# A fifth class of experts, for at most 64 rows, whose weights are multiplied unsplit in the expert stage of a diffusion step

## The chip, the cores and the metric

The kernel runs on one core of a Trainium2 chip. The time is the device time of one execution in microseconds (us). PE is TensorE, ACT ScalarE, DVE VectorE, POOL GpSimd, and SP the engine whose queue issues the weight loads.

## What is computed

Two layers over 384 rows of width 1024 (128 context rows, 256 latent rows), all in float32. Each layer has a token mixer and a channel mixer. The channel mixer of the first layer is a dense SwiGLU; that of the second is a choice of 2 of 8 experts, each a SwiGLU with inner width 2816:

```python
def swiglu(x, w_gu, w_d):
    g, u = jnp.split(x @ w_gu, 2, axis=-1)
    return (jax.nn.silu(g) * u) @ w_d

def moe_swiglu(x, w_router, w_gu, w_d):
    t = x.reshape(-1, D_MODEL)
    logits = (t @ w_router).astype(jnp.float32)
    top_v, top_i = lax.top_k(logits, TOP_K)
    gates = jax.nn.softmax(top_v, axis=-1)
    ...
    for e in range(N_EXPERTS):
        out = out + combine[:, e:e + 1] * swiglu(t, w_gu[e], w_d[e])
```

The 384 rows make 768 pairs of a row and an expert, so an expert has 96 rows on average, and its number is known only when the router has run.

## The kernel before

**The stream of weights.** All large weights come as one stream of 375 chunks of [128, 2048] float32, 1 MB each, in a fixed order (`STREAM`). SP loads chunk n into slot n % 6 of a ring of six (`raw`), with two DMAs, as soon as PE is done with chunk n - 6 (semaphore `s_pe`). An expert is 33 chunks: 22 of `w_gu` (`N_GU`; gate and up, in blocks of 512 columns, four chunks a block) and 11 of `w_d`. Chunks 111 to 374 of the stream are those of experts 0 to 7.

**Split products.** A float32 product is made of three products of the type float32r: ACT copies a chunk to float32r (`whi`, a ring of three), DVE subtracts that from the chunk in place (`wlo`), and PE multiplies whi by xhi, wlo by xhi and whi by xlo (the helper `three`, lines 1576 to 1578). The splits run two chunks or so ahead of PE (`upto`). The rows' own halves are `xhi`/`xlo` (and `hhi`/`hlo` for the hidden rows).

**Classes of experts.** The program holds each expert in each of four classes, `SHAPES`: (1, 0) is one tile of 128 rows; (1, 1) one tile and up to 32 more rows, the quarter, whose products PE makes unsplit in four column groups of the array (line 2105 for gate and up, 2138 for down); (2, 0) and (3, 0) two and three tiles. DVE counts the rows of each expert and writes the number of the class to `ntile`. PE, ACT and DVE each load it ahead of every expert and compare it with the classes (`by_tiles`). All eight experts of a class stand one behind the other in the program, so that an engine falls through to the next expert where the class stays, and jumps where it changes. The program is entered at the first class's expert 0.

**One expert.** POOL gathers its rows from `h_rows` to `hx`, PE turns them (`gathered`, at down chunks 4 and 6 of the expert before), ACT and DVE make `xhi` and `xlo` of them. Per block: gate and up products in PSUM, ACT's silu, DVE's product (`gated`), PE turns it (line 2072), ACT and DVE split it into `hhi` and `hlo`, and the down products add up over all 22 k-tiles. ACT copies the result to `f` (line 933; for the quarter DVE does), POOL scatters it to `y_rows` and gathers the rows of the expert after the next. `warm(n, bank)` (line 1588) issues n products of the identity with itself, which nothing reads.

## Time and profile before

| | us |
|---|---|
| median of 3 runs (lowest, highest) | 1615.28 (1614.29, 1617.17) |
| the profiled execution | 1618.33 |
| its span, first to last instruction | 1616.6 |
| PE, DVE, ACT busy in the span | 1557.5, 1031.7, 872.7 |
| moved by DMA | 425 MB, mean 263 GB/s |

The profiled execution is 3.05 us longer than the median. Its own span lies 1.7 us under its time. In the rows below, PE's matmuls are pipelined, so their spacing tells more than their length; a float32 product leaves two records in the trace and a split product one each. The chunks' names say nothing of their number, so experts are found by time: expert 0 starts at 759.5 us, expert 1 at 853.5, expert 2 at 947.4, expert 5 at 1228.2, expert 6 at 1321.8, expert 7 at 1459.1.

### The profile page before, as it was taken

The numbers are of one execution on the slowest core, as the hardware profiler recorded it, in microseconds if no ns is written. First come the engines' busy times: TensorE is split into PE (matmuls) and PEld (weight loads), VectorE is DVE, ScalarE is ACT, GpSimd is POOL, SyncE is SP. The second block draws the span as 40 slices with busy tenths as digits, with TensorE's granted clock in tenths as the row PEclk, the third lists the DMA queues.
The fourth block names the chain that finished last, engine by engine and source line by source line (L and its number), as shares of the span: only waits on it lengthen the run. The fifth ranks groups of instructions, "written<-read, shape, count | busy, mean of one in ns | idle before, by whom it ended". The sixth has DMA issues, their size and how long they took to land.

```text
span 1616.6 us, 24317 instructions
## 1 busy us (share of the span) xinstructions
PE 1557.5 (96%) x10076; PEld 1229.6 (76%) x10076; DVE 1031.7 (64%) x935; ACT 872.7 (54%) x886; POOL 164.9 (10%) x180
## 2 busy tenths in 40 slices
PE   6999999999999999998999999999999999999994
PEld 3677777777777778777888888888888878778872
DVE  1445574333422464557888889888888966666665
ACT  2435453222322454545777777777777755555553
POOL 2400000000000220012102030110303010001001
PEclk9999999999999999999999999999999999999998
DMA  9973325666665473233999999999999987878871
GB/s 330 335 264 143 94 84 170 222 210 211 229 241 201 126 246 112 85 125 129 381 371 382 383 367 387 372 379 376 379 383 372 388 323 254 272 265 302 271 283 69
DMA packets 214762, 425.02 MB, mean 263 GB/s; under 512 B 21986, under 2 KB 62946, under 8 KB 214528
## 3 DMA queue, kind: packets, MB, share of 16 engines
q1 hardware_dynamic: 200448, 397.99, 69.4%
q0 software_dynamic: 13056, 22.71, 4.7%
q10 hardware_dynamic: 1136, 2.64, 0.4%
q8 instruction: 84, 1.38, 0.4%
q14 instruction: 38, 0.31, 0.1%
HBM read 418.56 MB, written 22.41 MB: 273 GB/s over the span
## 4 chain that ended last, share of the span: by engine, by line
PE 90%; DVE 4%; DMA 2%; SPq 2%; ACT 1%; issue 1%; POOL 0%; DVEq 0%; ACTq 0%; POOLq 0%
PE ps L1576 26%; PE ps L1578 25%; PE ps L1577 25%; PE ps L2105 3%; PE ps L1620 2%; DMA raw<-in_w_in_dram 1%; SPq L542 1%; PE ps L2138 1%; PE ps L2072 1%; DVE wlo L1072 1%; PE ps L1736 1%; ACT whi L760 1%; PE ps L1767 1%; PE ps L1751 1%; DVE f L1166 1%
## 5 line engine op out<-in xcount | busy, mean ns | idle before, releaser
L1072 DVE TENSOR_TENSOR wlo<-raw,whi 128x2048 fp32r<-128x2048 f32 x327 | 745.4, 2289 | 319.2 <-ACT whi L760 228.1
L760 ACT ACTIVATE whi<-raw 128x2048 fp32r<-128x2048 f32 x327 | 626.6, 1918 | 448.2 <-PE ps L1578 222.1
L1576 PE MATMUL ps<-whi,xhi 128*128 128x512 f32 (+1 forms) x1352 | 538.1, 398 | 5.0 <-DVE xlo L1150 2.3
L1578 PE MATMUL ps<-whi,xlo 128*128 128x512 f32 (+1 forms) x1352 | 524.2, 388 | 0.0
L1577 PE MATMUL ps<-wlo,xhi 128*128 128x512 f32 (+1 forms) x1352 | 524.0, 388 | 0.0
L1576 PEld LDWEIGHTS ps<-whi,xhi 128*128 128x128 f32 x1352 | 255.2, 189 | 68.8 <-issue 15.1
L1578 PEld LDWEIGHTS ps<-whi,xlo 128*128 128x128 f32 x1352 | 255.1, 189 | 53.2
L1577 PEld LDWEIGHTS ps<-wlo,xhi 128*128 128x128 f32 x1352 | 255.5, 189 | 47.8 <-issue 0.5
L1576 PE MATMUL ps<-whi,hhi 128*128 128x512 f32 x484 | 193.9, 401 | 2.6 <-DVE wlo L1072 2.6
L1578 PE MATMUL ps<-whi,hlo 128*128 128x512 f32 x484 | 189.4, 391 | 0.0
L1577 PE MATMUL ps<-wlo,hhi 128*128 128x512 f32 x484 | 189.4, 391 | 0.0
L1576 PEld LDWEIGHTS ps<-whi,hhi 128*128 128x128 f32 x484 | 91.2, 189 | 24.1 <-issue 3.5
L1578 PEld LDWEIGHTS ps<-whi,hlo 128*128 128x128 f32 x484 | 91.3, 189 | 19.7
L1577 PEld LDWEIGHTS ps<-wlo,hhi 128*128 128x128 f32 x484 | 91.4, 189 | 18.1 <-issue 0.2
L734 POOL DMA_INDIRECT y_rows<-f,lidx x24 | 35.4, 1476 | 655.9 <-ACT f L933 400.4
L1620 PE MATMUL ps<-raw,cS 128*32 128x512 f32 x384 | 52.2, 659 | 15.5 <-DMA raw<-in_w_ada_dram 15.5
L709 POOL DMA_INDIRECT hx<-h_rows,lidx x21 | 44.3, 2111 | 9.4 <-issue 6.1
L1620 PEld LDWEIGHTS ps<-raw,cS 128*32 128x32 f32 x384 | 10.2, 114 | 43.2 <-issue 23.3
L905 ACT ACTIVATE hhi<-ps 128x512 fp32r<-128x512 f32 (+1 forms) x48 | 26.3, 548 | 26.9 <-PE ps L2072 13.6
L992 ACT ACTIVATE pr<-ps 128x512 f32<-128x512 f32 (+1 forms) x36 | 19.8, 557 | 37.6 <-PE ps L1578 37.5
L1110 DVE TENSOR_TENSOR f<-ps,f 128x512 f32<-128x512 f32 x12 | 8.3, 690 | 49.1 <-PE ps L1620 49.1
L2105 PE MATMUL ps<-raw,xsum 128*32 128x128 f32 x1280 | 39.0, 274 | 0.0
(245 smaller groups left out, 1090.2 us busy)
## 6 DMA issues: line engine op xcount, KB each, us to landing
raw<-in_w_moe_gu_dram SPq DMA_DIRECT2D x352, 512.0 KB, 5.6
raw<-in_w_moe_d_dram SPq DMA_DIRECT2D x176, 512.0 KB, 5.1
raw<-in_w_ada_dram SPq DMA_DIRECT2D x96, 512.0 KB, 5.1
raw<-in_w_in_dram SPq DMA_DIRECT2D x44, 512.0 KB, 5.3
raw<-in_w_ffn_gu_dram SPq DMA_DIRECT2D x44, 512.0 KB, 6.8
raw<-in_w_ffn_d_dram SPq DMA_DIRECT2D x22, 512.0 KB, 7.0
raw<-in_w_out_dram SPq DMA_DIRECT2D x16, 512.0 KB, 4.2
bias<-rpb_rows POOLq DMA_DIRECT2D x32, 96.0 KB, 4.9
```

The lines of the kernel that those rows point to most:

```text
L542: sp.dma_start(to, of).then_inc(s_raw[n % RING], 16)
L709: pool.indirect_dma_start(out=hx[:, i, :], out_offset=None, in_=h_rows[:, :], in_offset=bass.IndirectOffsetOnAxis(ap=lidx[:, e, i:i + 1], ...
L734: pool.indirect_dma_start(out=y_rows[:, :], out_offset=bass.IndirectOffsetOnAxis(ap=lidx[:, e, i:i + 1], axis=0), in_=f[:, i, :], in_offse ...
L760: act.activation(whi[m % SPL][:, :], raw[n % RING][:, :], ACT.Copy).then_inc(s_hi, 1)
L905: act.activation(hhi[:, kts.start:kts.stop, 0:P * T], ps[:, bank, 0:P * T * len(kts)].rearrange("p (k n) -> p k n", k=len(kts)), ACT.Copy) ...
L992: act.activation(pr[:, t, 512 * b:512 * b + width], ps[:, t, 0:width], ACT.Copy).then_inc(s_pr, 1)
L1072: dve.tensor_tensor(wlo[n % RING][:, :], raw[n % RING][:, :], whi[NTH[n] % SPL][:, :].bitcast(F32), ALU.subtract).then_inc(s_lo, 1)
L1576: pe.matmul(out, a_hi, w_hi, start=start, stop=False)
L1577: pe.matmul(out, a_hi, w_lo, start=False, stop=False)
L1578: return pe.matmul(out, a_lo, w_hi, start=False, stop=stop)
L1620: ins = pe.matmul(ps[32 * k:32 * k + 32, bank, :], cS[:, 4 * h + k, :], w[:, k, :], start=(h == 0), stop=(h == 1))
L2105: ins = pe.matmul(o, xsum[:, kt, P:P + QUARTER], m, start=(kt == 0 and i == 0), stop=(kt == KT - 1 and i == len(weights) - 1))
```

## The change

A fifth class, (0, 0), is put in front of the others, for experts with at most 64 rows. For these, ACT and DVE split only the expert's first two chunks (which the expert before has already done), and PE multiplies the rows by the chunks as they were loaded, in float32: each product has 64 stationary columns, and the two halves of a block's columns go to the two halves of the output partitions. The rows come unsplit as `xsum`, which DVE copies from PSUM. Behind each chunk but the first two stand two products of `warm`. The count of rows gets one more comparison. The two calls in which `T == 0` goes to `half_expert` are the same on all three engines.

The classes, and where a half expert's blocks lie:

```diff
-SHAPES = [(1, 0), (1, 1), (2, 0), (3, 0)]
+HALF = P // 2
+SHAPES = [(0, 0), (1, 0), (1, 1), (2, 0), (3, 0)]
...
+        DOWN_BANK = 4
+        def half_gated(b):
+            return gated[:, 256 * (b % 2):256 * (b % 2) + block_width(b) // 2]
+        def half_gate(b):
+            return ps[:, 2 * (b % 2), 0:block_width(b) // 2]
```

ACT:

```diff
+            def half_expert(e):
+                n0, k = PLACE["exp", e, 0], e + 1
+                act.sem_inc(s_morea, KT)
+                act.sem_inc(s_hhi, FK)
+                for b in range(LAST_BLOCK + 1):
+                    act.wait_ge(s_pe, n0 + gate_done(b) + 1)
+                    act.wait_ge(s_ht, FK * k + 4 * (b - 1) if b > 1 else FK * k)
+                    act.activation(half_gated(b), half_gate(b), ACT.Silu
+                                   ).then_inc(s_sg, units(b) - units(b - 1) if b else 2)
+                act.sem_inc(s_hi, N_FFN - 2)
+                state["n"] = n0 + N_FFN
...
+                upto(n0 + N_FFN + 1)
...
+                act.wait_ge(s_pe, n0 + N_FFN)
+                for j in range(2):
+                    ins = act.activation(f[0:HALF, 0, 512 * j:512 * j + 512],
+                                         ps[HALF * j:HALF * j + HALF, DOWN_BANK, :], ACT.Copy)
+                ins.then_inc(s_ye, 1)
...
             def expert(T, quarter, e):
+                if T == 0:
+                    return half_expert(e)
```

DVE, and the count of rows:

```diff
+            def half_expert(e):
+                n0, k = PLACE["exp", e, 0], e + 1
+                dve.wait_ge(s_glo, KT * (e + 1))
+                for i in range(2):
+                    ins = dve.tensor_copy(xsum[:, 4 * i:4 * i + 4, 0:HALF], gathered_banks(i)[:, :, 0:HALF])
+                ins.then_inc(s_mored, KT)
...
+                for b in range(LAST_BLOCK + 1):
+                    mult(b)
+                    copy(b)
+                dve.sem_inc(s_lo, N_FFN - 2)
...
-            chain(dve.tensor_scalar(cnt[:, :], ps[:, 3, 0:NE], float(P), None, ALU.is_gt))
+            chain(dve.tensor_scalar(cnt[:, :], ps[:, 3, 0:NE], float(HALF), None, ALU.is_gt))
+            chain(dve.scalar_tensor_tensor(out=cnt[:, :], in0=ps[:, 3, 0:NE], scalar=float(P), in1=cnt[:, :],
+                                           op0=ALU.is_gt, op1=ALU.add))
```

PE:

```diff
+            def half_expert(e):
...
+                def weights(c, k):
+                    n = n0 + c
+                    if c < 2:
+                        pe.wait_ge(s_lo, NTH[n] + 1)
+                        return [v.bitcast(F32) for v in halves(n, k)]
+                    pe.wait_ge(s_raw[n % RING], 32 * (n // RING + 1))
+                    return [raw[n % RING][:, :].rearrange("p (k n) -> p k n", k=k)]
+
+                def gate_up_chunk(c):
+                    b, part = divmod(c, 4)
+                    if c == 0:
+                        pe.wait_ge(s_mored, KT * (e + 1))
...
+                    ws = weights(c, 4)
+                    w = block_width(b) // 2
+                    for kk in range(4):
+                        kt = 4 * (part % 2) + kk
+                        for i, v in enumerate(ws):
+                            for j in range(2):
+                                rows = slice(HALF * j, HALF * j + HALF)
...
+                                ins = pe.matmul(o, xsum[:, kt, 0:HALF], m, start=(kt == 0 and i == 0),
+                                                stop=(kt == KT - 1 and i == len(ws) - 1))
+                    pe_done(ins)
+                    if c >= 2:
+                        warm(2, 5)
...
+                for q in range(FK // 2):
...
+                    w = weights(N_GU + q, 2)[0]
+                    for i in range(2):
+                        kt = 2 * q + i
+                        for j in range(2):
+                            ins = pe.matmul(ps[HALF * j:HALF * j + HALF, DOWN_BANK, :], hsum[:, kt, 0:HALF],
+                                            w[:, i, 512 * j:512 * j + 512], start=(kt == 0), stop=(kt == FK - 1))
+                    pe_done(ins)
+                    warm(2, 5)
```

The first place is PE at the end of the routing, where the first class's expert 0 begins (L2016 and L2104 pick the rows, L1576 to L1578 are split products, L2188 the new class's; this is before):

```order
L2016 MATMUL ps<-pick,f 128x128 x24
L500 TENSOR_LOAD ntile
L500 ISA x2
L520 COMPARE_AND_BRANCH x3
L1576 MATMUL ps<-whi,xhi 128x512
L1577 MATMUL ps<-wlo_52,xhi 128x512
L1578 MATMUL ps<-whi,xlo 128x512
```

And the same place of the change:

```order
L2104 MATMUL ps<-pick,f 128x128 x24
L516 TENSOR_LOAD ntile
L516 ISA x2
L536 COMPARE_AND_BRANCH x4
L2188 MATMUL ps<-whi,xsum 64x256 x2
L2188 MATMUL ps<-wlo_52,xsum 64x256 x2
L2188 MATMUL ps<-whi,xsum 64x256 x2
```

What stands behind the comparisons, and is reached without a jump, was the one-tile class and is now the class for at most 64 rows; the one-tile class begins 8 experts further on. There is one comparison more at each of these places.

The second place is PE in the new class, chunks 2 to 5 of an expert (L2188 the products, L1676 `warm`, L2152 the turned block):

```order
L2188 MATMUL ps<-raw,xsum 64x256 x8
L1676 MATMUL ps<-ident 128x128 x2
L2188 MATMUL ps<-raw,xsum 64x256 x8
L1676 MATMUL ps<-ident 128x128 x2
L2188 MATMUL ps<-raw,xsum 64x256 x8
L1676 MATMUL ps<-ident 128x128 x2
L2188 MATMUL ps<-raw,xsum 64x256 x8
L1676 MATMUL ps<-ident 128x128 x2
L2152 MATMUL ps<-ident,pg 128x128 x2
```

Twelve products of 512 columns a chunk have become eight of 256 and the two throwaway ones, and a block is turned by two products where four stood.

The third place is ACT in the new class, a whole expert up to the next (L905 silu, L895 the next expert's rows, L776 splits, L922 the output):

```order
L905 ACTIVATE pg<-ps 128x256 [waits s_ht,s_pe] x5
L905 ACTIVATE pg<-ps 128x128 [waits s_ht,s_pe]
L895 ACTIVATE xhi<-ps 128x4x128 [waits s_ga] x2
L776 ACTIVATE whi<-raw 128x2048 [waits s_pe,s_raw3]
L776 ACTIVATE whi<-raw 128x2048 [waits s_pe,s_raw4]
L922 ACTIVATE f<-ps 64x512 [waits s_yst,s_pe]
L922 ACTIVATE f<-ps 64x512
L516 TENSOR_LOAD ntile
L516 ISA x2
L536 COMPARE_AND_BRANCH x4
```

Of 33 splits an expert, two are left, those of the next expert's first chunks; they stand ahead of the copy of the output and of the comparisons, and every other split of the next expert stands behind them.

## Rows read from the trace of the kernel before

**Rows 1.** The page: busy time by engine, GB/s in 40 slices

```profile
PE 1557.5 (96%) x10076; PEld 1229.6 (76%) x10076; DVE 1031.7 (64%) x935; ACT 872.7 (54%) x886; POOL 164.9 (10%) x180
GB/s 330 335 264 143 94 84 170 222 210 211 229 241 201 126 246 112 85 125 129 381 371 382 383 367 387 372 379 376 379 383 372 388 323 254 272 265 302 271 283 69
```

**Rows 2.** Stretches: us, PE, PEld, DVE, ACT, POOL busy, PEclk, DMA share, GB/s

```profile
853.50:947.40 93.90, 93.67 (x427) 77.15 (x426) 82.67 (x48) 70.50 (x48) 10.47 (x6) 1.00 1.03 378
1324.80:1331.20 6.40, 6.35 (x20) 4.73 (x20) 0.42 (x1) 1.91 (x1) 5.00 (x5) 0.51 0.73 243
1331.20:1459.10 127.90, 127.90 (x1369) 100.07 (x1369) 83.00 (x59) 68.58 (x52) 0.00 (x0) 1.00 0.76 259
```

**Rows 3.** Waits of SP's queue: us in total, times, longest

```profile
SPq L542 <- PE ps L1578: 1159.6, 319, 28.3
```

**Rows 4.** Timeline of PE from expert 1 to 2: start, us, what

```profile
947.00 0.39 PE L1578 MATMUL ps<-whi,hlo 128*128 128x512 f32 x1
947.22 0.39 PE L1576 MATMUL ps<-whi,xhi 128*128 128x512 f32 x1
```

**Rows 5.** DMA of 876:896, 907:917, 930:947, software queue of 853:947

```profile
DMA packets 4006, 7.73 MB, mean 387 GB/s; under 512 B 234, under 2 KB 234, under 8 KB 4005
DMA packets 1098, 4.00 MB, mean 400 GB/s; under 512 B 122, under 2 KB 122, under 8 KB 1098
DMA packets 2708, 6.00 MB, mean 353 GB/s; under 512 B 188, under 2 KB 188, under 8 KB 2708
q0 software_dynamic: 864, 0.84, 2.7%
```

**Rows 6.** DMA, software queue of 948.5:958 and of 1146:1153

```profile
q0 software_dynamic: 288, 0.23, 7.3%
q0 software_dynamic: 407, 0.16, 8.8%
```

**Rows 7.** Timeline of PE in layer 1 and ahead of the router

```profile
150.74 1.15 PE L1781 MATMUL ps<-pr,pT 128*64 128x64 f32 x32
733.12 5.07 PE L1588 MATMUL ps<-ident 128*128 128x128 f32 x44
```

**Rows 8.** Timeline of DVE, an operation of the routing's count

```profile
751.18 0.17 DVE L1535 TENSOR_SCALAR lg<-ps 128x8 f32<-128x8 f32 x1
```

**Rows 9.** Timelines of PE and ACT, expert 5 to 6, [idle before]

```profile
1324.85 1.06 PE L2032 MATMUL ps<-ident,hx 32*128 32x32 f32 x8 [3.13 <-issue]
1326.43 0.63 PE L1577 MATMUL ps<-wlo,xhi 128*128 128x512 f32 x1
1326.86 0.63 PE L1578 MATMUL ps<-whi,xlo 128*128 128x512 f32 x1
1327.53 1.91 ACT L760 ACTIVATE whi<-raw 128x2048 fp32r<-128x2048 f32 x1 [4.75 <-issue]
```

**Rows 10.** Timelines of ACT and PE behind expert 7

```profile
1592.74 1.28 ACT L818 ACT_TABLE_LOAD   x1 [1.79 <-issue]
1591.79 1.12 PE L1920 MATMUL ps<-gate_f,selb 128*128 128x512 f32 x2 [1.90 <-DVE f L1315]
```

**Rows 11.** Timelines of PE, ACT and DVE at the start of expert 0

```profile
759.50 0.50 PE L1576 MATMUL ps<-whi,xhi 128*128 128x512 f32 x1 [1.54 <-DVE xlo L1203]
759.38 1.92 ACT L760 ACTIVATE whi<-raw 128x2048 fp32r<-128x2048 f32 x1 [0.74 <-issue]
762.25 2.29 DVE L1072 TENSOR_TENSOR wlo<-raw,whi 128x2048 fp32r<-128x2048 f32 x1 [1.45 <-ACT whi L760]
```

**Rows 12.** A stretch of the first stage, columns as in rows 2

```profile
31.00:37.40 6.40, 6.40 (x32) 4.64 (x35) 3.00 (x7) 1.43 (x4) 0.00 (x0) 0.50 1.05 387
```

**Rows 13.** SP's issues of expert 6's chunks 0 and 6, chunk 0's landing

```profile
1307.68 0.89 SPq L542 DMA_DIRECT2D raw<-in_w_moe_gu_dram  x2
1334.98 0.88 SPq L542 DMA_DIRECT2D raw<-in_w_moe_gu_dram  x2
raw<-in_w_moe_gu_dram SPq DMA_DIRECT2D x2, 512.0 KB, 5.3
```

More of the change, by code:

```diff
@@ L477, in gated_part, with half_up @@
             return gated[:, 0:block_width(b)] if T == 1 else f[:, t, 0:block_width(b)]
+        DOWN_BANK = 4
[3 more added lines that the diff above has]
+            return ps[:, 2 * (b % 2), 0:block_width(b) // 2]
+        def half_up(b):
+            w = block_width(b) // 2
+            return ps[:, 2 * (b % 2) + 1, 0:w] if b < LAST_BLOCK else ps[:, 2 * (b % 2), w:2 * w]
         def rest_width(b):
@@ L1252, in near_sum, with mult, copy @@
                                          in1=hx[:, t, :], op0=ALU.mult, op1=ALU.add).then_inc(s_near_d, 1)
+            def half_expert(e):
[4 more added lines that the diff above has]
+                ins.then_inc(s_mored, KT)
+                def mult(b):
+                    dve.wait_ge(s_sg, GU_B * k + units(b))
+                    dve.wait_ge(s_pe, n0 + up_done(b) + 1)
+                    dve.tensor_tensor(half_gated(b), half_gated(b), half_up(b), ALU.mult
+                                      ).then_inc(s_pm, units(b) - units(b - 1) if b else 2)
+                def copy(b):
+                    n = ktiles(b) // 2
+                    dve.wait_ge(s_hhi, FK * (k + 1))
+                    dve.wait_ge(s_ht, FK * k + 4 * b + ktiles(b))
+                    for i in range(n):
+                        ins = dve.tensor_copy(hsum[:, 4 * b:4 * b + 2 * n, 0:HALF].rearrange("p (j i) n -> p i j n", i=n)[:, i],
+                                              ps[:, 6 + b % 2, P * i:P * i + P].rearrange("p (j n) -> p j n", j=2))
+                    ins.then_inc(s_hlo, ktiles(b))
+                for b in range(LAST_BLOCK + 1):
+                    mult(b)
+                    copy(b)
+                dve.sem_inc(s_lo, N_FFN - 2)
+                state["n"] = n0 + N_FFN
+                for q in range(FK // 2):
+                    if e < NE - 1 and q in GATHER_AT:
+                        gathered(e + 1, GATHER_AT[q])
+                    if e == NE - 1 and 7 <= q < 7 + NT:
+                        near_sum(q - 7)
+                upto(n0 + N_FFN + 1)
             def expert(T, quarter, e):
+                if T == 0:
+                    return half_expert(e)
                 n0, k = PLACE["exp", e, 0], e + 1
@@ L2054, in expert @@
             def expert(T, quarter, e):
+                if T == 0:
+                    return half_expert(e)
                 n0, k = PLACE["exp", e, 0], e + 1
```

46 lines of the change are left out of this document (added).

## The prediction

> **What bounds the kernel now.** The page first: PE is busy 96% of the span and the chain that ended last is 90% PE [rows 1]. From 740 us on, the 40 slices show a full PE beside 370 to 390 GB/s, so two resources may be full at once. The view by stretches settles this [rows 2]. Expert 1 lasts from 853.5 to 947.4, 93.9 us; in it PE is busy 93.67 us at the full granted clock, and the DMA share is 1.03 at 378 GB/s. For comparison, the stretch of expert 6, where PE has more to do per byte, shows share 0.76 at 259 GB/s: there the DMA engines idle, in expert 1 they hardly do. SP waits for PE to free a ring slot [rows 3], so PE sets the pace, but narrowly.
>
> How narrowly, per 1 MB chunk (1.0486 MB). PE: a gate or up chunk is 12 split products 0.227 us apart [rows 4], 2.72 us; with transposes 93.9 / 33 = 2.85 us. DMA: in a stretch of gate and up chunks the queue is never empty and moves 387 GB/s, 2.71 us a chunk; in one of w_down chunks 400 GB/s, 2.62 us [rows 5]. So 22 x 2.71 + 11 x 2.62 = 88.4 us. The rows that are scattered and gathered come on top: for expert 1 the software queue moved 0.84 MB [rows 5], 2.2 us at 387, and contention about them roughly doubles that (estimate). Floor 92 to 93 us against 93.9. **The loads have 1 to 1.5 us of slack per expert**: in the last 17 us before 947 the rate was 353 instead of about 390 GB/s [rows 5], 17 x (1 - 353/390) = 1.6 us, the only idle of that expert; I take 1.3.
>
> **Which experts change class.** The scatter of expert 1's results moved 0.23 MB, 55 rows of 4 KB; the gather for expert 5 0.16 MB, 38 rows [rows 6]. The router's counts worked out from the reference's inputs agree: 98, 55, 106, 107, 71, 38, 158, 135. Two of eight are halves, apart from each other, so the order of classes becomes full, half, full, full, full, half, quarter, quarter. Expert 0 is no longer of the class that the program falls into.
>
> **Cost of a half chunk on PE.** 8 float32 products of 256 columns (w_down: 4 of 512), each recorded as two matmuls. Nearest rows: 32 records of 64 columns in two column groups took 1.15 us from first start to last end; less the last one's 0.22, 0.030 us a record, where 64 columns at two cycles each are 0.053 [rows 7]. So two groups do run side by side. 16 records of 256 columns at two cycles are 16 x 0.213 / 2 = 1.71 us. The two throwaway products are four records of 0.115 us (44 took 5.07 us [rows 7]), 0.46 us. Together 2.17 us a chunk, under the 2.6 to 2.7 us of its load. Chunks 0 and 1 keep their split and multiply both parts, 3.42 us each. So **a half expert is bound by the loads**: 24 us less work on PE can return only the 1.3 us of idle DMA, and what lead the landed chunks had over PE. ACT and DVE lose 31 splits of 1.92 and 2.29 us there, which were beside the path.
>
> **Terms of the sum** (+ is later), followed through the program:
>
> 1. Routing: one more chained DVE operation, 0.2 us as its neighbours are spaced [rows 8]. +0.2.
> 2. Expert 0 is now reached by a taken jump. The trace has two taken jumps. Into expert 6, with busy DMA engines, PE stood 3.13 us and ACT 4.75 us with "issue" as releaser [rows 9]; at the end, with idle DMA engines, ACT 1.79 and PE 1.90 us [rows 10]. Expert to expert within a class PE runs on without a gap [rows 4]. At expert 0 ACT's split of chunk 2 began at 759.38 after 0.74 us idle, and DVE ended it at about 764.54, just before PE wants it at 765.1 [rows 11]. The jump adds 1 us (1.79 - 0.74) to 4 us (4.75 - 0.74); nearer the idle case, but not idle (the h_rows scatters run): 2.4, of which 0.5 was cover. +2.0 (0.5 to 3.5).
> 3. Into expert 1: PE jumps, and DVE jumps before it copies xsum, which PE now waits for. PE stopped at about 853.5 and restarts at 853.5 + 3.1 to 5 = about 858. In the jump into expert 6 the granted clock fell to 0.51 while PE stood, and the next products came 0.43 us apart for 6.4 us [rows 2, 9]; I take the same, to about 863. Chunk 0 (3.42 us of work) then ends at 864 and chunk 1 at 867.4, where PE now ends them 2.72 us apart, at 856.2 and 858.9. A slot is only refilled then. The DMA engines had two chunks and the scatter left, 6.5 us, so they run dry at 860 and get data again at 864 + 2.2 (5 us from issue to landing [rows 13] less 2.7 of transfer): 5.6 us idle with the second slot's gap. The gather for expert 2, part of the 0.84 MB, falls into that hole and gives back 1.6. +4.0 (0.5 to 6).
> 4. Rest of expert 1: the stream of loads uses its idle. PE gains 0.5 us a chunk and is level with it at the end. -1.3.
> 5. Into expert 2: PE must wait for landing, ACT and DVE, 4.3 us, which hides its own jump. ACT copies the output after its two splits, then jumps (4.75): chunk 2 is split about 5 us after it could be. But the scatter and gather fall on an expert's first ten chunks and put their landing about 4 us behind PE's pace (the extra of the floor above), which covers most. +0.8 (0 to 3).
> 6. Experts 3 and 4: PE's pace as now. 0.
> 7. Expert 5, as terms 3 and 4: +4.0 - 1.3.
> 8. Into expert 6: its first chunk is issued at 1307.68 and lands at about 1314; PE resumes only at 1324.85 [rows 9], since it was behind and then jumped, and frees the slot at 1334.98 [rows 13], 21 us after landing. After a half PE is not behind: 4.3 us for the split, 5.2 at the low clock, 3.8 for the quarter's part behind DVE's jump, some 13.7. This is where all the saved work comes out. -7.2 (-10 to -4).
>
> Sum 0.2 + 2.0 + 4.0 - 1.3 + 0.8 + 4.0 - 1.3 - 7.2 = **+1.2 us**. The profiled execution took 1618.33 us (span 1616.6), so 1619.5 there. It stands 3.05 us above the median of the runs, 1615.28; on that scale I forecast **1616.5**. What a measurement can tell from no change is 0.2%, 3.2 us.
>
> The jump term has a rule that speaks against the change. The rows say that a taken jump costs PE about 3 us and ACT up to 4.75 [rows 9]. The Trainium skill, "Runtime: NRT & Kernel Launch", Instruction fetch mechanics, says that instructions are prefetched in sequence only and that a taken branch outside the two blocks at hand stalls on a DMA fetch. By this rule ACT's and DVE's jumps, over few instructions in the new class, could sometimes stay inside, and only PE's would always pay; terms 2, 3 and 5 would be nearer their low ends and the sum about -4.
>
> **Rivals.**
> - *Cheap jumps, faster.* ACT and DVE find their code at hand and PE's gap of some 3 us does not bring the clock down. Against it: it fell in a gap of 3.13 us [rows 9]. For it: behind PE's gap of 1.54 us before expert 0 the first product is recorded with 0.50 us [rows 11], where those at the low clock have 0.63 [rows 9]. Terms 2, 3, 5 and 7 become 0.5, 0.5, 0, 0.5: 0.2 + 0.5 + 0.5 - 1.3 + 0.5 - 1.3 - 7.2 = -8.1, 1607. It decides when each entry costs the load stream under 2 us. Chance 0.18 for all below 1612.
> - *Entries cost more, slower.* Mechanism: the throttle holds through the two doubled chunks. If the clock also falls at expert 0 (a gap of 3 us, then chunks at 0.43 spacing) that costs about 3, and entries at the high bound 2 each more: +8, 1623. Chance 0.27.
> - *The clock falls again and again in a half expert.* PE would work 2.17 of 2.7 us. At half clock a chunk is 4.3 us and puts PE 1.6 behind; a ring of six absorbs one fall, not one in every second stretch. In the first stage, where PE also waits for loads, the clock fell and stood at 0.50 for 6.4 us with a full DMA queue [rows 12]. Price: mean 3.0 us a chunk, 31 x 0.3 x 2 = +18, 1634. Chance 0.10.
> - *Two groups of 256 columns don't overlap.* Then 3.42 + 0.46 = 3.9 us a chunk, 66 x 1.05 = +70, 1685. Rows 7 speak against it. Chance 0.01.
>
> **How the numbers follow.** The forecast, within 1612 to 1619, has 0.44. Range 1608 to 1628: it takes in the cheap jumps and the dear entries, and leaves out the repeated falls and the far ends. Faster by over 0.2%: 0.18. Slower: the last three, 0.38. Within: 0.44. The forecast's own range is 1612 to 1619.
>
> **What would show it.** In the changed trace: experts 1 and 5 about 93 us long with the DMA share still near 1.0 and PE busy near 75 us; idle of PE, releaser "issue" or the DVE copy, of 3 to 5 us at the entries of 1, 2, 5, 6 and a new one before 0; granted clock at 0.5 behind each; a drop of the GB/s for some 5 us near 862 and 1240; between PE's end of expert 5 and its first products of 6 about 5 us. Wrong would be: half experts well under 90 us (the loads go faster than 387 to 400 GB/s with more of them under way, about which the rows of a full queue say no), or PE 100% busy in them.

## The result, and the profile after

The changed kernel took 1629.8 us (median of 4 runs, 1628.38 to 1631.2) beside 1614.85 us of the kernel before (1614.29 to 1617.17): ratio 1.009, 95% interval 1.0072 to 1.0107. It is slower. The forecast of 1616.5 and its range up to 1628 both missed. The profiled execution took 1630.04 us with a span of 1628.3, 11.7 us more than the span before.

The page of the changed kernel, busy time by engine and GB/s in 40 slices, answers to [rows 1]:

```profile
PE 1553.6 (95%) x10454; PEld 1179.0 (72%) x10454; DVE 889.9 (55%) x888; ACT 748.8 (46%) x814; POOL 151.3 (9%) x180
GB/s 329 332 274 130 98 89 158 234 215 212 233 244 167 140 255 117 53 124 154 366 369 322 392 375 379 361 383 375 380 383 310 384 393 249 272 265 312 262 289 68
```

DVE lost 142 us of work and ACT 124, PE 4. Two slices in the expert stage fell to 322 and 310 GB/s: the entries to experts 1 and 5.

SP's issues of chunk 5 of each expert happen as PE ends the expert before; the rows are the ends of experts 0, 1, 2, 4, 5 and 6 in the changed kernel:

```profile
858.21 0.37 SPq L558 DMA_DIRECT2D raw<-in_w_moe_gu_dram  x1
951.82 0.37 SPq L558 DMA_DIRECT2D raw<-in_w_moe_gu_dram  x1
1051.79 0.37 SPq L558 DMA_DIRECT2D raw<-in_w_moe_gu_dram  x1
1239.62 0.37 SPq L558 DMA_DIRECT2D raw<-in_w_moe_gu_dram  x1
1333.36 0.37 SPq L558 DMA_DIRECT2D raw<-in_w_moe_gu_dram  x1
1471.18 0.37 SPq L558 DMA_DIRECT2D raw<-in_w_moe_gu_dram  x1
```

Before, they stood at 853.49, 947.42, 1041.00, 1228.16, 1321.75 and 1459.12. So the lateness is 4.7, 4.4, 10.8, 11.5, 11.6, 12.1 us, and 0.4 is regained by the end of the span. Read this way, experts 1 and 5 themselves are as long as before; the time is lost ahead of the end of expert 0 (4.7 us) and **in expert 2, behind the first half expert** (6.4 us more). Expert 6 adds only 0.5, because there a loss of the same kind meets the return of term 8.

PE's waits of the changed kernel, whole span (total, times, longest), cut to the expert stage:

```profile
PE ps L2188 <- DVE xsum L1306: 9.5, 2, 5.1
PE ps L1664 <- DVE wlo L1119: 7.6, 4, 4.2
...
PE ps L2120 <- issue: 4.0, 1, 4.0
PE ps L1664 <- issue: 3.7, 1, 3.7
```

These are the entries to experts 1 and 5 (L2188), 2 (4.2 us), 6 (L2120) and 0. Before there were 3.1 us at expert 6 [rows 9] and 1.5 at expert 0 [rows 11]. PE's and DVE's timelines at expert 0 and expert 1 of the changed kernel:

```profile
762.13 0.76 PE L1664 MATMUL ps<-whi,xhi 128*128 128x512 f32 x1 [3.67 <-issue]
763.64 1.91 ACT L776 ACTIVATE whi<-raw 128x2048 fp32r<-128x2048 f32 x1 [4.48 <-issue]
862.43 0.75 DVE L1306 COPY xsum<-ps 128x256 f32<-128x256 f32 x2 [2.64 <-issue]
863.24 1.12 PE L2188 MATMUL ps<-whi,xsum 128*64 128x256 f32 x4 [5.07 <-DVE xsum L1306]
```

At expert 1 PE stood 5.07 us until 863.24, because DVE, which had jumped too, reached its copy only at 862.43. DVE had ended its last split at 857.50 + 2.29 = 859.79, so 2.64 us is only the part in which it waited for nothing else.

The trace also has the comparisons that PE's queue makes ahead of an expert. The one that jumps lasts until PE can go on with the code it jumps to. For the jump into expert 1, by source line (PEldq is PE's queue), and the record of the first instruction of the new class (at experts 1 and 5):

```profile
L536 PEldq COMPARE_BRANCH  x1: 4370/4370/4370, 855.3 to 855.3; - x1
L2193 PEldq EVENT_SEMAPHORE  x2: 51/51/51, 859.7 to 1242.2; - x2
```

So PE's queue met the comparison at 855.3, 2.9 us before PE's last queued product ended at 858.18, and stood 4.37 us in it. PE had its new code back at 859.7: **of the 5.07 us of idle, 1.5 are PE's own jump and 3.5 the wait for DVE's copy.** The DMA view of just this stretch (855.28 to 859.65) shows one transfer of the queue of instructions:

```profile
q8 instruction: 1, 0.02, 1.4%
```

The five jumps into experts 0, 1, 2, 5 and 6 held PE's queue for 4.0, 4.4, 6.2, 5.5 and 6.3 us, and before, the jump into expert 6 for 6.0. What PE itself stands of that is less by the products already queued: 0.7 us of them at expert 0, 2.9 behind a full expert, 2.3 behind a half one.

Stretches of the changed kernel, columns as in [rows 2]: experts 1 and 5 whole, and the first us behind two entries:

```profile
858.20:951.80 93.60, 88.56 (x612) 49.40 (x612) 9.69 (x23) 6.48 (x11) 6.02 (x6) 0.96 0.98 363
863.20:867.60 4.40, 4.36 (x22) 2.42 (x24) 0.00 (x0) 0.00 (x0) 3.48 (x4) 0.50 0.57 179
1239.60:1333.30 93.70, 89.25 (x612) 49.74 (x612) 9.24 (x23) 6.32 (x10) 6.00 (x6) 0.96 0.99 364
1338.70:1342.10 3.40, 3.40 (x8) 2.73 (x9) 0.08 (x1) 1.91 (x1) 2.48 (x4) 0.50 1.04 378
```

The granted clock was 0.50, the lower of the two levels (1.2 GHz), behind each of the five entries and nowhere inside a half expert. Behind the entry to expert 1 the DMA share fell to 0.57: the five next chunks have landed, and no slot comes free while PE stands and then works at half the clock. The GB/s of that place in 40 slices of 0.15 us (861 to 867 us) show the loads running dry and what is left, POOL's transfers of rows:

```profile
GB/s 410 396 355 341 314 314 355 369 410 369 396 396 423 492 369 423 342 328 247 232 111 125 70 28 55 55 55 55 55 1 0 137 82 55 55 273 246 410 437 382
```

ACT's first splits for experts 2 and 6 of the changed kernel start as their chunk lands:

```profile
948.94 1.91 ACT L776 ACTIVATE whi<-raw 128x2048 fp32r<-128x2048 f32 x1 [5.86 <-DMA raw<-in_w_moe_gu_dram]
1330.90 1.91 ACT L776 ACTIVATE whi<-raw 128x2048 fp32r<-128x2048 f32 x1 [6.29 <-DMA raw<-in_w_moe_gu_dram]
```

Before, these chunks landed at 938.3 and 1314.1 (the trace's records of the queue), so the loads are 10.6 and 16.8 us later, more than PE.

Inside a half expert, PE's timeline at its chunks 3 and 4 (the first row is the part of chunk 3 that the view's window takes in, the last of chunk 4):

```profile
875.73 1.03 PE L2188 MATMUL ps<-raw,xsum 128*64 128x256 f32 x8
876.69 0.71 PE L1676 MATMUL ps<-ident 128*128 128x128 f32 x4
877.33 0.87 PE L2188 MATMUL ps<-raw,xsum 128*64 128x256 f32 x6
```

From one to the next of such places is 2.5 us. The throwaway products, with the changes of shape around them, hold the next chunk up by 877.33 - 876.69 = 0.64 us, where 0.46 had been forecast, and about 0.2 more passes ahead of them. In the trace the eight products of a chunk take 1.73 us (forecast: 1.71).

### The profile page after: what moved, and what is told of

The parts are those of the page before. It is cut to its first block, busy times and chain, and to the rows that moved or that the text cites. A ratio compares the mean times of both kernels' runs of the same rounds, so it can differ in the third digit from the quotient of the medians.

```text
span 1628.3 us, 24862 instructions
## 1 busy us (share of the span) xinstructions
PE 1553.6 (95%) x10454; PEld 1179.0 (72%) x10454; DVE 889.9 (55%) x888; ACT 748.8 (46%) x814; POOL 151.3 (9%) x180
## 3 DMA queue, kind: packets, MB, share of 16 engines
q10 hardware_dynamic: 1136, 2.64, 0.4%
q8 instruction: 94, 1.54, 0.4%
## 4 chain that ended last, share of the span: by engine, by line
PE 87%; DVE 5%; DMA 4%; issue 2%; ACT 1%; SPq 1%; DVEq 0%; POOL 0%; POOLq 0%; ACTq 0%
PE ps L1664 21%; PE ps L1666 21%; PE ps L1665 20%; PE ps L2188 6%; PE ps L2271 3%; PE ps L1676 2%; PE ps L1708 2%; PE ps L2206 2%; DMA raw<-in_w_in_dram 1%; PE ps L2304 1%; DMA raw<-in_w_moe_gu_dram 1%; ACT whi L776 1%; DVE wlo L1119 1%; PE ps L2238 1%; PE ps L1824 1%
## 5 line engine op out<-in xcount | busy, mean ns | idle before, releaser
L1119 DVE TENSOR_TENSOR wlo<-raw,whi 128x2048 fp32r<-128x2048 f32 x265 | 604.0, 2290 | 317.3 <-ACT whi L776 224.6
L776 ACT ACTIVATE whi<-raw 128x2048 fp32r<-128x2048 f32 x265 | 507.9, 1918 | 433.8 <-PE ps L1666 204.4
L1664 PE MATMUL ps<-whi,xhi 128*128 128x512 f32 (+1 forms) x1176 | 470.3, 400 | 11.1 <-DVE wlo L1119 5.0
L1666 PE MATMUL ps<-whi,xlo 128*128 128x512 f32 (+1 forms) x1176 | 456.3, 388 | 0.0
L1665 PE MATMUL ps<-wlo,xhi 128*128 128x512 f32 (+1 forms) x1176 | 456.3, 388 | 0.0
L1664 PEld LDWEIGHTS ps<-whi,hhi 128*128 128x128 f32 x396 | 74.8, 189 | 20.9 <-issue 3.5
L1676 PEld LDWEIGHTS ps<-ident 128*128 128x128 f32 x428 | 55.6, 199 | 34.3 <-issue 34.1
L2188 PE MATMUL ps<-raw,xsum 128*64 128x256 f32 x640 | 77.8, 385 | 0.0
L1676 PE MATMUL ps<-ident 128*128 128x128 f32 x428 | 68.1, 299 | 0.0
L905 ACT ACTIVATE pg<-ps 128x256 f32<-128x256 f32 (+1 forms) x12 | 4.4, 366 | 123.9 <-PE ps L2188 123.9
L2188 PEld LDWEIGHTS ps<-raw,xsum 128*64 128x64 f32 x640 | 42.5, 137 | 22.6 <-issue 1.3
L2206 PE MATMUL ps<-raw,hsum 128*64 128x512 f32 x176 | 42.6, 605 | 0.0
```

Of the source, the lines that this page charges most:

```text
L776: act.activation(whi[m % SPL][:, :], raw[n % RING][:, :], ACT.Copy).then_inc(s_hi, 1)
L1119: dve.tensor_tensor(wlo[n % RING][:, :], raw[n % RING][:, :], whi[NTH[n] % SPL][:, :].bitcast(F32), ALU.subtract).then_inc(s_lo, 1)
L1664: pe.matmul(out, a_hi, w_hi, start=start, stop=False)
L1665: pe.matmul(out, a_hi, w_lo, start=False, stop=False)
L1666: return pe.matmul(out, a_lo, w_hi, start=False, stop=stop)
L1676: pe.matmul(ps[:, bank, NT * P:NT * P + P], ident[:, :], ident[:, :], start=True, stop=True)
```

## The experiments

The kernel before took 1614 us on one chip and 1622.5 us on two others (the result's own chip is not known; its time goes with the first). So each kernel is compared with the kernel before on its own chip, by ratio; 0.1% is 1.6 us.

| kernel | median us | before there | ratio (95%) |
|---|---|---|---|
| no expert half | 1620.66 | 1613.95 | 1.004 (1.0027, 1.0052) |
| other order | 1622.99 | 1613.95 | 1.0045 (1.003, 1.006) |
| twin class | 1631.18 | 1613.95 | 1.0103 (1.0086, 1.012) |
| no throwaway products | 1626.33 | 1613.95 | 1.0079 (1.0066, 1.0092) |
| classes fixed, changed | 1622.59 | 1622.62 | 1.0001 (0.9992, 1.001) |
| classes fixed, before | 1622.67 | 1622.62 | 1.0003 (0.9993, 1.0012) |
| first part only | 1630.02 | 1622.62 | 1.0042 (1.003, 1.0054) |
| combined | 1624.05 | 1622.62 | 1.0007 (0.9997, 1.0017) |
| changed kernel again | 1633.83 | 1622.42 | 1.0072 (1.0059, 1.0084) |
| fixed and combined | 1621.41 | 1622.42 | 0.9995 (0.9984, 1.0006) |
| early rows | 1631.45 | 1622.42 | 1.0063 (1.0051, 1.0075) |

### No expert half: the jump to expert 0 alone

```diff
-            chain(dve.tensor_scalar(cnt[:, :], ps[:, 3, 0:NE], float(HALF), None, ALU.is_gt))
+            chain(dve.tensor_scalar(cnt[:, :], ps[:, 3, 0:NE], 0.0, None, ALU.is_gt))
```

> The class for at most 64 rows stays in the program, but the first count comparison is with 0 rows, so no expert falls into it. Against the kernel before there is left: the comparison, and that expert 0 is reached by a jump and not fallen into. Theory (code not at hand): the jump of PE costs 2 us there and DVE's some 5 us, so that the split of chunk 2 is late and everything behind expert 0 is 4.7 us later: 1614.9 + 4.7 = about 1619.5; in the trace expert 1 starts at 858.2, and the entries to experts 1, 2 and 5 show no gap. Rival (the changed kernel's loss is that of the products of the new class): under 1 us, about 1615.5.

Ratio 1.004, 6.5 us (4.4 to 8.4); the theory's 4.7 lies in it, the rival's 1 does not. PE's and DVE's timelines at expert 0:

```profile
759.67 0.76 PE L1664 MATMUL ps<-whi,xhi 128*128 128x512 f32 x1 [3.76 <-issue]
765.00 6.69 DVE L1119 TENSOR_TENSOR wlo<-raw,whi 128x2048 fp32r<-128x2048 f32 x3 [6.24 <-issue]
```

DVE's split of chunk 2 came behind 6.24 us of idle with nothing to wait for, where it was 1.45 us behind ACT before [rows 11]. The entries to 1, 2 and 5 had no gap. Its expert 1 began at 855.69, 2.2 us late and not 4.7, but the routing ahead of it ends at another time in each execution (the last product that picks rows ended at 757.95 before, 758.46 in the changed kernel, 755.91 here). Counted from there, expert 0 ended after 95.5 us before, 99.75 in the changed kernel and 99.8 here: the jump costs 4.2 us in both. One trace doesn't show the whole 6.5: the jump into expert 6 took only 1.82 us in it, with no low clock behind it, and the profiled execution of the kernel before was 3 us over its median.

### Other order: expert 0 fallen into again

```diff
+ORDER = [2, 1, 3, 4, 5]
...
-            leave(1, 0)
-            for kind, shape in zip(kinds, SHAPES):
+            leave(ORDER[0], 0)
+            for kind in ORDER:
+                shape = SHAPES[kind - 1]
```

> The changed kernel with the new class put behind the one-tile class in the program, so that expert 0 is fallen into again; all else as in the changed kernel. Theory (code not at hand): 4.5 us less than the changed kernel, 1629.8 - 4.5 = about 1625.3, and the first chunk of expert 0 done at about 762.8. Rival (the delay at expert 0 is that of the comparison or of the loads, or whatever is won there is taken back by the entry to expert 1, where the loads have more lead): 1628 to 1630.

Ratio 1.0045, 7 us better than the changed kernel's 1.009 (4 against the 1.0072 of its second measurement). PE's gaps at experts 0, 1 and 5:

```profile
761.17 0.50 PE L1666 MATMUL ps<-whi,xhi 128*128 128x512 f32 x1 [1.54 <-DVE xlo L1252]
860.11 1.12 PE L2190 MATMUL ps<-whi,xsum 128*64 128x256 f32 x4 [4.97 <-DVE xsum L1308]
1238.83 0.65 PE L2190 MATMUL ps<-whi,xsum 128*64 128x256 f32 x4 [2.35 <-DVE xsum L1308]
```

The first is back at 1.54 us, as in [rows 11]. The third is half of what it was (4.46), with no low clock behind it. PE's queue stood 4.5 us in its comparison there (5.5 in the changed kernel, 4.4 in its second trace), and DVE's copy followed its last split without a gap (1.6 us behind DVE's comparison, 3.7 in both traces of the changed kernel): DVE's jump above all became cheaper, with the same code ahead and behind and only its place in the program changed. That part of the gain had not been expected.

### Twin class: the jumps without the unsplit products

```diff
-SHAPES = [(0, 0), (1, 0), (1, 1), (2, 0), (3, 0)]
+SHAPES = [(1, 0), (1, 0), (1, 1), (2, 0), (3, 0)]
```

> The changed kernel with the new class's code replaced by a twin of the one-tile class: experts 1 and 5 jump in and out as in the changed kernel, but all their products are split. Theory (the entries cost, the unsplit products give some back): expert 0 +4.7, and the entries to experts 1, 2 and 5 each a gap of PE of 3 to 4 us and 3.4 to 6.8 us at half the clock (1.7 to 3.4 us lost), 5 to 7 us each, so 4.7 + 15 to 21 = about 20 to 26 over the kernel before, 1635 to 1641; the changed kernel is then 5 to 11 better than its twin. Rival (the new class's products are what costs): at most 8 over the kernel before, 1623 or less, so better than the changed kernel.

Ratio 1.0103, 16.6 us (13.9 to 19.4): under the theory's 20, but far over the rival's 8. Less the 6.5 of expert 0, the entries to 1, 2 and 5 cost about 10 us, with gaps of 3.6, 2.7 and 1.9 us in the trace. **By these ratios the unsplit products give back 2 us (1.0103 less 1.009) to 5 us (less the 1.0072 of the second measurement)**; against 1.009 the intervals overlap, and 5 to 11 had been expected.

### No throwaway products

```diff
-                    if c >= 2:
-                        warm(2, 5)
...
-                    warm(2, 5)
```

> The changed kernel without the two throwaway products behind each chunk of the new class. Theory (they keep nothing up, and the changes between 64 and 128 columns cost PE 0.2 us each time): a chunk takes PE 1.73 us and not 2.51, PE is done with experts 1 and 5 some 3 us sooner behind the last landing, and experts 2 and 6 begin that much sooner: 1629.8 - 3 to 6 = about 1625. Rival (they hold the clock up): PE is busy 64% of the time, the granted clock falls to 0.5 inside experts 1 and 5, a chunk takes 3.4 us at that clock, more than its load, and the time is 10 to 40 us more, 1640 to 1670.

Ratio 1.0079: 1.8 us better than 1.009 and 1.1 worse than the 1.0072 of the second measurement, so a gain is likely (3.5 us by the medians 1626.33 and 1629.8) but not shown; 3 to 6 had been expected. The rival's loss of 10 to 40 us fell. Stretches inside experts 1 and 5:

```profile
868.00:946.00 78.00, 64.61 (x459) 32.68 (x457) 6.42 (x19) 3.40 (x8) 0.00 (x0) 1.00 1.02 380
1245.00:1323.00 78.00, 64.19 (x455) 32.35 (x453) 6.42 (x19) 3.39 (x8) 0.00 (x0) 1.00 1.03 379
```

PE was busy 64.6 of 78 us (idle 17%) and the clock stayed at 1.00 (2.4 GHz): in this kernel the throwaway products keep no clock up. PE is done with expert 1 in 90.6 us instead of 93.6. Its gap at the next entry grows by 1.2 us, though expert 2 as a whole takes as long as in the changed kernel (99.6 and 100.0). PE and ACT at the entry to expert 2:

```profile
952.22 0.76 PE L1664 MATMUL ps<-whi,xhi 128*128 128x512 f32 x1 [5.41 <-DVE wlo L1119]
947.45 1.91 ACT L776 ACTIVATE whi<-raw 128x2048 fp32r<-128x2048 f32 x1 [9.63 <-DMA raw<-in_w_moe_gu_dram]
```

Two waits end there at nearly the same time: the split of the chunk that landed at 947.4 (DVE done at 951.7), and PE's own jump. Its queue met the comparison at 945.7 and stood in it for 6.2 us, until 951.9, as long as with the throwaway products; but only 1.1 us of queued products lay in front, where there had been 2.3. At expert 6 the chunk was ready before PE's jump was over, and the gap was the jump alone, 5.4 us instead of 4.0.

### Classes fixed in the program, of the changed kernel and of the kernel before

```diff
...
-            leave(1, 0)
-            for kind, shape in zip(kinds, SHAPES):
-                for e in range(NE):
-                    nc.switch_bb(label(kind, e), parent=entry)
-                    part(*shape, e)
-                    leave(kind, e + 1)
...
+            for e, shape in enumerate([(1, 0), (0, 0), (1, 0), (1, 0), (1, 0), (0, 0), (1, 1), (1, 1)]):
+                part(*shape, e)
```

> The changed kernel with the classes of these eight experts written into the program (one tile, half, one tile three times, half, quarter twice) and no comparisons or jumps: each engine's instructions stand one behind the other. It gives the right output for this input only. Theory (the jumps cost, the unsplit products by themselves gain): against the kernel before with its own classes fixed in the same way (the next kernel), which I expect at 1608, each half expert now returns most of the 8 us by which its first chunk has landed ahead of PE, less 2 to 3 us for its first two chunks of double work: 4 to 5 each, about 1599. Rival (the unsplit products don't pay even so, since the loads bound them): within 2 us of the next kernel.

> The kernel before with the classes fixed in the same way: experts 0 to 5 one tile, 6 and 7 quarter, no comparisons or jumps. Theory: the gap of 3.1 us into expert 6, the low clock behind it (some 2.6 us in the executions that have it) and part of the gap of 1.9 us at the end go: 1614 - 5 to 7 = about 1608. Rival (a jump into the quarter's class is hidden, the gap there is a wait for rows): 1613 to 1614.

Both came out as the kernel before (1.0001 and 1.0003). Two expectations fell. First, without any jump the half class returns nothing: the rival. (It still waits for the copy of the rows and multiplies both parts of its first two chunks.) Second, the kernel before gains nothing when its jump into expert 6 goes. PE's waits of the fixed kernel before, in expert 6, say why:

```profile
PE ps L2080 <- issue: 3.4, 6, 1.0
```

The 3.1 us of the jump [rows 9] are gone, and 3.4 us of waits for nothing shown, up to 1 us each, stand between the 128 short products of the quarter's first chunk, with no jump anywhere near. So what a jump costs at this place another wait takes, of the same releaser "issue", where many short products follow each other. The Trainium skill, "Runtime: NRT & Kernel Launch", Instruction fetch mechanics, says that instructions come by DMA in blocks, in sequence, and that a fetch in sequence is mostly hidden while a taken branch stalls. The jumps agree: each of the 53 branches of PE that jump, in all traces, lasted 3.3 to 6.3 us and has a transfer of 16 KB by the queue of instructions within it. The fixed kernel's 3.4 us are another matter: the only such transfer near ran from 1324.5 to 1325.5 us, and the two longest waits, of 1.0 us each, ended at 1326.75 and 1328.18, with none beside them. What they wait for stays open.

### First part only

```diff
-                        return [v.bitcast(F32) for v in halves(n, k)]
+                        return [v.bitcast(F32) for v in halves(n, k)[:1]]
```

> The changed kernel, but a half expert's chunks 0 and 1 are multiplied by their first part (whi) alone, which leaves out the products with wlo: 8 products and not 16 for each of the two chunks, everything else as in the changed kernel. Theory (behind an entry the first slots come free late because the doubled chunks run at half the clock): chunk 0 is done 3.4 us sooner at the entries to experts 1 and 5 and chunk 1 up to 5 us, so that the hole in the loads shrinks by 3 to 5 us each: 1629.8 - 6 to 9 = about 1622. Rival (the hole is set by the gap of PE alone, and whatever is won is lost to the full DMA engines afterwards): 1627 to 1630.

The edit leaves out the products with wlo for chunks 0 and 1. Ratio 1.0042 against 1.0072 and 1.009 of the changed kernel, 5 to 8 us: the theory. PE's gaps at experts 1 and 5 were 4.95 and 4.93 us (5.07 and 4.46 in the changed kernel), so the gain is not theirs. (The median in us, 1630, is that of a chip on which the kernel before takes 1622.6.) The double work on the two chunks that the expert before had already split, just where a late slot starves the loads, is a cost of its own, of the size of the jump's.

### Early rows

```diff
                 dve.tensor_tensor(xlo[:, k, 0:P], gathered_banks(i), xhi[:, k, 0:P].bitcast(F32), ALU.subtract
-                                  ).then_inc(s_glo, 4)
+                                  )
+                dve.tensor_copy(xsum[:, k, 2 * P:2 * P + HALF], gathered_banks(i)[:, :, 0:HALF]).then_inc(s_glo, 4)
...
-                dve.wait_ge(s_glo, KT * (e + 1))
...
-                ins.then_inc(s_mored, KT)
+                dve.sem_inc(s_mored, KT)
...
-                        pe.wait_ge(s_mored, KT * (e + 1))
+                        pe.wait_ge(s_glo, KT * (e + 1))
```

> The changed kernel with one edit: the unsplit rows are copied by DVE while the expert before still runs, so that PE waits at an entry for its own jump alone. Theory (PE's own jump takes 3.1 to 4.2 us, as at experts 2 and 6): the gaps at experts 1 and 5 become about 4, the time 1 to 2 us less than the changed kernel's on the same chip. Rival (the gaps of 5.1 and 4.5 us were DVE's jump, and PE finds its code in under 2 us, as in the combined version, where its gap at expert 1 was 1.7 us): gaps of about 1.8, less time at the low clock, 5 to 9 us less than the changed kernel.

1.0063 against 1.0072 on the same chip: 1.5 us by the ratios and 2.4 by the medians, near the theory's 1 to 2, but the intervals overlap, so the gain is not shown. PE's gaps at experts 1, 2 and 5:

```profile
859.14 1.12 PE L2187 MATMUL ps<-whi,xsum 128*64 128x256 f32 x4 [3.21 <-issue]
953.08 0.76 PE L1663 MATMUL ps<-whi,xhi 128*128 128x512 f32 x1 [4.14 <-DVE wlo L1119]
1238.66 0.65 PE L2187 MATMUL ps<-whi,xsum 128*64 128x256 f32 x4 [2.10 <-DVE wlo L1119]
```

Both gaps at the half experts shrank, to 3.2 and 2.1 us, and neither became the theory's 4. What is left is PE's own jump. At expert 5 its queue stood 4.7 us in the comparison, and 1.8 us of that was idle: the rival's size, and the low clock did not follow. At expert 1 it stood 5.8 us, where it had been 4.4 in the changed kernel, so that 2.9 us were idle; that this is near the 3.13 of [rows 9] is chance. The rival was right that the gap of the changed kernel at expert 1 was mostly DVE's (3.5 of 5.1 us), and wrong that 5 to 9 us would come of it.

### Combined, and combined with fixed classes

The new class behind the one-tile class, early rows, no throwaway products; then the same with fixed classes (diffs as above).

> The version that the first runs point to: the new class behind the one-tile class in the program, no throwaway products, and the unsplit rows copied by DVE while the expert before still runs (behind the split of the rows, into columns of xsum of their own), so that PE waits at an entry for no copy behind DVE's jump. Theory (terms add up): against the changed kernel -6 to -7 for the order, -2 to -3 for the throwaway products, -1.4 for the copy: 1618 to 1620, still 4 to 6 over the kernel before, since PE's own gaps of 3 to 4 us at experts 1, 2 and 5 and the low clock behind them stay. Rival (the loads take back what PE wins): 1621 to 1623. Below 1614 only if the gaps are no cost.

> Classes fixed for this input as before (right for this input only), with the unsplit rows copied early and without the throwaway products. Theory (the half class by itself returns nothing with fixed classes because of its own entry: a wait of 2.3 us for the copy of the rows and two chunks of double work; take the copy's wait away and a return shows): 3 to 5 us, 0.2 to 0.3%, under the kernel before. Rival (a half expert's length is set by its loads, whatever its entry does): within 0.1% of the kernel before.

Combined: 1.0007, as fast as the kernel before within 0.17%, better than its expectation (4 to 6 us over). Nearly all of the loss is removed, and nothing is won. With fixed classes 0.9995, the rival's result (within 0.1%); the theory's 0.2 to 0.3% lies outside the interval, 0.9984 to 1.0006. The fixed one's stretches (expert 1, then expert 2), PE's waits in expert 1, and ACT's first split of expert 2:

```profile
855.80:942.60 86.80, 69.58 (x491) 36.24 (x490) 8.63 (x22) 4.98 (x10) 6.02 (x6) 1.00 1.02 381
942.60:1041.80 99.20, 95.42 (x427) 78.46 (x428) 86.39 (x51) 73.76 (x51) 14.19 (x6) 0.98 1.04 381
```

```profile
PE ps L2164 <- DMA raw<-in_w_moe_gu_dram: 10.5, 14, 1.8
PE ps L2180 <- DMA raw<-in_w_moe_d_dram: 5.1, 9, 0.6
```

```profile
942.00 1.91 ACT L753 ACTIVATE whi<-raw 128x2048 fp32r<-128x2048 f32 x1 [9.63 <-DMA raw<-in_w_moe_gu_dram]
```

Expert 1 is 7 us shorter (86.8), with 23 waits of PE for landings at a DMA share of 1.02, and expert 2 then 5.6 us longer (99.2 against 93.6). Its first chunk lands 942.00 - 855.8 = 86.2 us after expert 1 began. In the kernel before that took 84.8 us: the stream of loads is no earlier, so what PE wins in expert 1 it waits in expert 2. Over the pair 1.5 us are won (186.0 against 1041.0 - 853.5 = 187.5), and over experts 5 and 6, by the same count, 3.0 (228.0 against 231.0). Expert 0 gives 1.9 of that back: in both combined versions it ends 97.4 us after the last product that picks rows, where it was 95.5. DVE's new copy stands ahead of expert 0's first product there, PE's gap is 1.80 us instead of 1.54, and the granted clock was 0.50 for the 3.4 us behind it, where it had been 1.00. So this trace has a small return of the half experts, hidden by a cost of the early copy at expert 0; a version without that cost was not run.

### The kernels again on another chip

> The kernel before once more, one look, on the chip of these four kernels. The runs that were taken with the two kernels of fixed classes had the kernel before at 1622.6, not 1614, and in their traces the first two chunks of expert 7, whose class is not entered by a jump, took PE 10.2 and 7.0 us with waits of 0.3 us each for nothing shown, against 7.5 and 4.7 in the first trace of the kernel before. If that belongs to the chip and not to the kernels, the time here is either near 1614 with 7.5 and 4.7, or near 1622 with about 10 and 7.

> The changed kernel once more, to have it beside the others on one chip: 0.9% over the kernel before if the difference belongs to the kernels (0.72 to 1.07% was measured); the gaps of PE at the entries again 3.7, 5.1, 4.2, 4.5 and 4.0 us within 0.5 each.

The kernel before took 1623.52 us here and the changed one 1.0072 times that chip's median, with gaps of 3.7, 5.0, 4.2, 4.5 and 4.1 us: the loss belongs to the kernel. PE's waits in the first two chunks of expert 7 (not jumped into), kernel before on this chip:

```profile
PE ps L2105 <- issue: 2.4, 8, 0.3
```

In the first trace of the kernel before this row does not exist. Up to expert 7 the two agree within 0.2 us (1458.94 and 1459.12); the 5.2 us by which the spans differ lie in expert 7 and behind it. From the end of expert 6 to the end of the span it was 157.1 to 158.0 us in the six traces taken with the kernel before at 1614 to 1615 us, and 162.4 to 163.1 in the eight taken with it at 1622.5: this goes with the chip and not with the kernel.

## Why the prediction was wrong, by its own terms

Lateness by stretch, from the ends above:

| terms | forecast | measured |
|---|---|---|
| 1 and 2, up to expert 1 | +2.2 | +4.7 |
| 3 to 5, experts 1 and 2 | +3.5 | +6.1 |
| 6, experts 3 and 4 | 0 | +0.7 |
| 7 and 8, experts 5 and 6 | -4.5 | +0.6 |
| the rest | 0 | -0.4 |
| sum | +1.2 | +11.7 |

**A reading behind several terms.** The prediction took the 3.13 us of idle [rows 9] for what a jump costs PE. The same trace has PE's queue in that comparison for 6.0 us, of which 2.9 lay under queued products. Where fewer are queued, behind a half expert and at expert 0, more of the jump shows.

**Term 2 was mis-sized.** It went through ACT's jump alone, at 2.4 us less 0.5 of cover, and put PE's own jump and DVE's at nothing; the low clock behind it stood only in a rival. PE stood 3.67 us instead of 1.54 and then met the low clock: expert 0's first chunk was done at 766.60 instead of 762.56, 4.0 us late (0.5 of it from the routing, whose end moves more than that from run to run, so that term 1's 0.2 can't be seen). DVE's jump ran beside that: its split of chunk 2 came some 5 us late (767.5 against 762.25 [rows 11]), and added 0.9 more there. That the jump to expert 0 is what costs is shown by no expert half (+6.5, 4.4 to 8.4) and by the other order (-4 to -7).

**Terms 3 and 4: PE's part right, the loads' part wrong.** PE's first chunk was forecast to be done 10.5 us behind the end of expert 0 (864 less 853.5); it was 10.9 (869.11 less 858.21). What failed is "5.6 us idle with the second slot's gap". Chunk 5 landed at 865.1 and chunk 6, issued at 869.11, at 874.4: 6.6 us more than the 2.7 of a full queue, and the next four together 2.2 us more, since PE frees slots 1 to 4 one at a time and none is in reserve. That is 8.8 us over a full queue for five chunks, where the kernel before had 2.8 in the same place: 6.0 us are new, where the term had 4.0. The landings were 10.2 us later than before at chunk 6, 11.0 at chunk 10, and still 10.6 at the end of the expert: **the 1.3 us of term 4 did not come back either**, only 0.3, since by the median a chunk of gate and up landed every 2.72 us and one of w_down every 2.56, and before every 2.71 and 2.55. The two together were forecast at +2.7 and were 10.6 - 4.7 = +5.9. First part only (5 to 8 us for two entries) shows that a good part of this hole is made by the double work at the entry.

**Term 5** (+0.8) came out at about 0.2, by another way. ACT's jump into expert 2 cost nothing; PE's own did. PE's counted products of expert 1 ended 2.9 us behind the landing, two throwaway products took 0.6 more, and the rest of its jump 4.2, so that it began 7.7 us behind the landing, not 4.3, and met the low clock. From landing to first chunk done were 12.2 us, and 11.9 before: at expert 2 a half expert in front returned nothing.

**Term 7** is terms 3 and 4 again: forecast +2.7, measured +5.3 (the landing of expert 6's first chunk 16.8 us late, expert 5's start 11.5).

**Term 8: mechanism right, size wrong.** From landing to first chunk done was forecast at 13.7 us and was 1346.9 - 1330.9 = 16.0, where it had been 20.9: a return of 4.9 and not 7.2. The step that failed is PE being ready when the split was, "4.3 us for the split". PE trailed the last load (a half chunk took 2.5 us and not 2.17), had its counted products done 2.5 us behind the landing and the throwaway ones 0.6 later. Its queue met the comparison only 0.8 us behind the landing and stood in it 6.3 us, of which 4.0 were idle: 7.1 us from landing to restart. From there to the first chunk done were 8.9 us, and 9.0 had been forecast (5.2 and 3.8).

**What held.** In the changed kernel half experts were bound by their loads and as long as expert 1 had been (93.6 and 93.7 us against 93.9; in other versions 86.9 to 92.4, with the next expert the longer); two column groups ran side by side (the rival of 1685 fell); the clock did not fall inside a half expert, with or without throwaway products (1634 fell). The outcome is the rival "entries cost more", forecast at 1623 with 0.27: right in mechanism (the clock did fall at expert 0, and the entries cost more), still too small. Cheap jumps, the faster rival, fell at experts 0, 1 and 2; at expert 5 gaps of 1.9 to 2.4 us did occur in other versions. PE's own share of them was 1.6 to 1.8 us, and what was gone was mostly the wait for DVE. That jumps of ACT and DVE might be nearly free was seen for both at expert 2 only.

**Left open.** The traces show which engine's jump and which queued products make up a gap, but not why PE's queue stands 4.4 us in one comparison and 6.2 in another, nor why DVE's jump took under 1.6 or 3.7 us at the same place. A version with both first chunks multiplied once and exactly was not tried. The shares of order and second parts, 4 to 7 and 5 to 8 us, already add up to the loss or more, so they may overlap; those of throwaway products (0 to 3) and of rows (2) are within the noise.

## What to carry to other kernels

Where the DMA engines already run at a share of 1.0 in a stage, less work on the compute engines can only shift waiting time to the next stage; price the gain by how much earlier the next stage's first load lands, not by busy time. A branch is paid by every engine that takes it, at the one whose jump comes last in the chain of waits, and the code's order in the program decides who pays: put the commonest class first (expert 0's, here), and move data that the entry needs ahead of the branch where that delays nothing else. What an engine stands at a jump is the jump less the work it had queued behind the comparison, so an idle reading understates the jump. At an entry the critical resource is the first ring slot: extra work on the first chunks, above all at a low clock, became a hole in the loads.

## What the runs showed of the hardware

- A branch that jumps held PE's queue for 3.3 to 3.9 us at the end (idle DMA engines) and for 3.9 to 6.3 us at the experts, each time with a transfer of 16 KB by the queue of instructions in it. In the changed kernel, from ACT's comparison to its next instruction it was 0.25 us into expert 1 and 4.0 into experts 0 and 5, and for DVE 0.3 us into expert 2 and 3.7 to 5.0 into experts 0, 1 and 5.
- At expert 5 PE stood 4.5 us in the changed kernel, 2.35 with the other order, 2.1 with early rows and 1.9 us in the twin; the one-tile code ahead of the jump was the same in all but for the early copy.
- Waits with no releaser shown appear without jumps: 3.4 us in 6 waits of up to 1.0 us among 128 short products in the fixed kernel before.
- The same kernel differed by 8 us between chips (1614 and 1622.5), 5.2 us of it from expert 7 on, with 2.4 us in eight waits of 0.3 us with no releaser shown, which the other chip did not have.
- Two changes between products of 64 and of 128 stationary columns cost a half chunk about 0.35 us: 2.51 us a chunk, less 1.73 for the products and four records of about 0.11.
- Behind an entry with a gap of 3.1 us or more the granted clock was 0.50 in every trace. Behind smaller gaps it varied: 2.35 and 2.1 us at expert 5 were followed by 1.00, 2.1 us at expert 6 (the kernel before again), 2.7 at expert 2 and 2.2 at expert 6 (twin) and 1.8 at expert 0 (combined) by 0.50. Inside experts 1 and 5 without throwaway products it stood at 1.00 throughout.
